# Quartered first loads and a swapped-operand gate product in a three-layer sequence-256 kernel

## The reference, cut to what matters

```python
proj = x @ w_in                      # x: 256 x 1024, w_in: 1024 x 8208
h_a, c_a, b_a, z_a, qkv, z_b, beta_raw, a_raw = jnp.split(proj, cuts, axis=-1)
qkv = jax.nn.silu(causal_depthwise_conv(qkv, conv_b_w))
beta = jax.nn.sigmoid(beta_raw)      # 8 columns, one for each head
g = -jnp.exp(a_log) * jax.nn.softplus(a_raw + dt_bias)   # 8 more columns
```

## Time and profile before

| what | value |
|---|---|
| runs | 1047.58, 1049.68, 1049.87 us (median 1049.68) |
| span of the profiled execution | 1048.4 us |
| what lies around the span | no separate time of the profiled execution is given; the median stands 1.28 us above its span |
| TensorE matmul / weight load busy | 97% / 86% of the span |
| VectorE / ScalarE busy | 72% / 51% |
| mean granted TensorE clock | 0.994 |

### The profile page before, as it was taken

The page is one execution under the profiler, slowest core; times in us unless marked ns, Lnnn a source line. Parts: engine busy times, 40 slices in busy tenths (PEclk is TensorE's granted clock), DMA queues, the critical chain, the costliest instruction groups (busy, mean ns, idle before and its releaser), DMA issues.

```text
span 1048.4 us, 21565 instructions
## 1 busy us (share of the span) xinstructions
PE 1019.6 (97%) x9120; PEld 897.6 (86%) x9120; DVE 752.1 (72%) x1049; ACT 530.2 (51%) x590; POOL 0.5 (0%) x7
## 2 busy tenths in 40 slices
PE   9999999999999999999999999989999999999998
PEld 7999999999866798989898787659986669999986
DVE  5999957678557668677787866867986775565553
ACT  5674544483353464435555433656687564335331
POOL 0000000000000000000000000000000000000000
PEclk8999999999999999999999999999999999999999
DMA  9454343244326664425343554876352446545441
GB/s 353 162 183 161 129 154 106 97 162 161 123 81 255 236 240 167 150 83 200 122 162 122 178 185 163 320 295 241 123 181 99 161 143 260 218 184 188 157 171 47
DMA packets 26302, 181.47 MB, mean 173 GB/s; under 512 B 3040, under 2 KB 3296, under 8 KB 4960
## 3 DMA queue, kind: packets, MB, share of 16 engines
q1 hardware_dynamic: 25056, 174.66, 45.2%
q10 hardware_dynamic: 1152, 5.45, 1.4%
HBM read 179.04 MB, written 1.05 MB: 172 GB/s over the span
## 4 chain that ended last, share of the span: by engine, by line
PE 87%; DVE 7%; ACT 3%; DMA 2%; issue 1%; SPq 0%; DVEq 0%; ACTq 0%
PE PS L916 84%; DVE WL L1799 2%; DMA RAW<-wst 1%; ACT WH L1386 1%; PE PS L1079 1%; DMA layer<-xt 1%; DVE X L1995 1%; DVE X L1996 1%; PE PS L1157 1%; PE PS L1307 0%; DVE STAT L1977 0%; DVE X L1976 0%; DVE layer_ln L2109 0%; DVE layer L2102 0%; ACT block L1690 0%
## 5 line engine op out<-in xcount | busy, mean ns | idle before, releaser
L916 PE MATMUL PS<-XTH,WH 128*128 128x256 f32 x1392 | 403.7, 290 | 6.2 <-issue 1.5
L916 PE MATMUL PS<-XTL,WH 128*128 128x256 f32 x1392 | 394.8, 284 | 0.0
L916 PE MATMUL PS<-XTH,WL 128*128 128x256 f32 x1392 | 394.7, 284 | 0.0
L1799 DVE TENSOR_TENSOR WL<-RAW,WH 128x2048 fp32r<-128x2048 f32 x138 | 314.2, 2277 | 99.8 <-ACT WH L1386 96.4
L1386 ACT ACTIVATE WH<-RAW 128x2048 fp32r<-128x2048 f32 x138 | 262.7, 1904 | 214.2 <-PE PS L916 208.7
L916 PEld LDWEIGHTS PS<-XTH,WH 128*128 128x128 f32 x1392 | 267.8, 192 | 12.6 <-issue 3.8
L916 PEld LDWEIGHTS PS<-XTL,WH 128*128 128x128 f32 x1392 | 268.0, 193 | 1.6 <-issue 1.4
L916 PEld LDWEIGHTS PS<-XTH,WL 128*128 128x128 f32 x1392 | 267.8, 192 | 0.0
L916 PE MATMUL PS<-WH,YH 128*128 128x512 f32 x224 | 89.6, 400 | 1.1 <-DVE YL L2274 1.1
L916 PE MATMUL PS<-WH,YL 128*128 128x512 f32 x224 | 87.4, 390 | 0.0
L916 PE MATMUL PS<-WL,YH 128*128 128x512 f32 x224 | 87.3, 390 | 0.0
(11 more groups left out here) (293 smaller groups left out, 1112.6 us busy)
## 6 DMA issues: line engine op xcount, KB each, us to landing
RAW<-wst SPq DMA_DIRECT2D x162, 1024.0 KB, 4.9
LNW<-lnrow ACTq DMA_DIRECT2D x3, 1024.0 KB, 6.7
RAW<-wst SPq DMA_DIRECT2D x4, 512.0 KB, 5.7
layer<-xt SPq DMA_DIRECT2D x2, 512.0 KB, 5.3
XR<-x ACTq DMA_DIRECT2D x1, 1024.0 KB, 4.7
out<-X SPq DMA_DIRECT2D x4, 256.0 KB, 3.3
CST<-cst ACTq DMA_DIRECT2D x1, 640.0 KB, 8.7
PT<-pt SPq DMA_DIRECT2D x1, 512.0 KB, 5.6
```

Of the source, the lines that this page charges most:

```text
L916: return pe.matmul(o, lhsT, rhs, start=start, stop=stop)
L1799: tt(WL[:, i % RAW_RING, 0:n], RAW[:, i % RAW_RING, 0:n], as_float(WH[:, k % SPLIT_RING, 0:n]), ALU.subtract).then_inc(vector_done, 1)
```

## The change

The diff changes the following things.

1. x and slab 0 are loaded in eight pieces of 256 KB (four each, in turn) in place of four of 512 KB. `xs` has four steps, and slab 0 is split by `top:0`, `top:1`, `top:2` and `split:0:0`. Unit k:0:0 waits for the pieces one by one.
2. The gate product is two steps. `baw` holds the gate weights still (two blocks side by side, 32 columns) in four column groups, with 512 columns of x moving: four float32 matmuls into PSUM bank 0, each output group a partial sum. ScalarE copies it to `BAW`. `ba` then adds up and transposes it by four float32 matmuls with `BAW` stationary and a 0/1 matrix `PICK` of 16 columns moving, into bank 1. `PICK` is made by VectorE in the new step `pick` by two `tensor_reduce` over parts of `ident`, behind a wait for `CST`.
3. `baw` is TensorE's first step, `ba` stands behind `k:0:0`. On VectorE the order is `xs:3 split:0:0 split:1:1 split:2:2 pick ba k:0:0 split:3:3 ba1`; before it was `xs:0 ba split:1:1 split:2:2 ba1 k:0:0 split:3:3`.
4. Four matmuls of ones in place of six.
5. `ORDER_T` is a new sequence all through the kernel. `ORDER_S` and `ORDER_V` are the same as before behind the front (VectorE's from `split:3:3` on but for `ba1`).

```diff
     step("setup", on="SGV")
-    for half in range(2):
-        step("xs", half, on="SV")
+    step("pick", on="V")
+    for q in range(4):
+        step("xs", q, on="SV")
...
-    step("ba", on="TV", banks=(0,))
+    step("baw", on="TS", banks=(0,))
+    step("ba", on="TV", banks=(1,))
...
 ORDER_T = """
-ba first:k:0:0 k:0:0 first:k:0:1 k:0:1 first:v:0:0 v:0:0 norm:k:0 first:v:0:1 first:q:0:0 v:0:1 gcc q:0:0 first:q:0:1
-q:0:1 first:zb:0:0 zb:0:0 gc:0 first:zb:0:1 zb:0:1 first:k:1:0 k:1:0 norm:q:0 vtr:0 first:k:1:1 k:1:1 first:v:1:1
...
-ab:0:1 gv:0:0 ah:1:0 gx:0:5:1 gs:0 first:ac:1:0 gu:0:6:1 gks:0 ac:1:0 gv:0:1 first:az:1:0 go:0 az:1:0 gr:0:0
-first:zb:1:0 first:ab:1:0 ab:1:0 zb:1:0 gc:1 first:ah:1:1 first:zb:1:1 zb:1:1 vtr:1 norm:q:1 first:ac:1:1 ah:1:1
...
-gu:1:3:0 gp:1:3:1 gx:1:2:1 gx:1:3:0 gp:1:4:0 gu:1:3:1 gu:1:4:0 gp:1:4:1 gx:1:3:1 gx:1:4:0 gp:1:5:0 gu:1:4:1 gu:1:5:0
...
-hm:0:6 first:q1:1:0 hc:0 q1:1:0 ho:0 first:q1:1:1 q1:1:1 hr:0:0 hd:1 first:i:1:0 first:f:2:0 i:1:0 first:i:1:1 hm:1:0
-first:f:2:1 hm:1:1 i:1:1 f:2:0 hm:1:2 f:2:1 hm:1:3 first:z1:1:0 z1:1:0 hm:1:4 first:z1:1:1 z1:1:1 first:q1:2:0 hm:1:5
...
-gate:1:0:1 first:gate:1:1:0 adat:6 first:gate:1:1:1 gate:1:1:0 gate:1:1:1 ada:7:0 ada:7:1 ada:9:0 ada:9:1 ada:4:0
-adat:7 xt:4:1 xt:4:0 xt:4:2 xt:4:3 adat:9 ada:4:1 first:feat:8 gates:0 feat:8 gates:1 first:feat:0 qn:1:2 gcol feat:0
...
+baw first:k:0:0 k:0:0 ba first:k:0:1 k:0:1 first:v:0:0 v:0:0 first:v:0:1 norm:k:0 v:0:1 first:q:0:0 gcc first:q:0:1
+gc:0 q:0:0 q:0:1 first:zb:0:0 zb:0:0 first:zb:0:1 zb:0:1 first:k:1:0 k:1:0 norm:q:0 vtr:0 first:k:1:1 k:1:1 first:v:1:0
...
+gp:0:6:1 ab:0:1 gv:0:0 ah:1:0 gs:0 gu:0:6:1 first:ac:1:0 gks:0 ac:1:0 gv:0:1 first:az:1:0 go:0 az:1:0 gc:1 gr:0:0
+first:ab:1:0 ab:1:0 first:zb:1:0 zb:1:0 first:zb:1:1 zb:1:1 first:ah:1:1 first:ac:1:1 vtr:1 norm:q:1 ah:1:1 ac:1:1
...
+gx:1:2:1 gp:1:3:1 gx:1:3:0 gp:1:4:0 gu:1:3:1 gu:1:4:0 gx:1:3:1 gp:1:4:1 gx:1:4:0 gp:1:5:0 gu:1:4:1 gu:1:5:0 gx:1:4:1
...
+hm:0:6 first:q1:1:0 hc:0 q1:1:0 ho:0 first:q1:1:1 q1:1:1 hr:0:0 hd:1 i:1:0 first:i:1:0 first:i:1:1 first:f:2:0 hm:1:0
+i:1:1 hm:1:1 first:f:2:1 f:2:0 hm:1:2 f:2:1 hm:1:3 first:z1:1:0 z1:1:0 hm:1:4 first:z1:1:1 z1:1:1 hm:1:5 first:q1:2:0
...
+gate:1:0:1 first:gate:1:1:0 adat:6 first:gate:1:1:1 gate:1:1:0 gate:1:1:1 ada:7:0 ada:9:0 ada:7:1 ada:9:1 adat:7
+ada:4:0 xt:4:1 xt:4:0 xt:4:3 xt:4:2 ada:4:1 adat:9 first:feat:8 gates:0 feat:8 gates:1 first:feat:0 qn:1:2 gcol feat:0
...
-            for half in range(2):
-                k, n = slice(4 * half, 4 * half + 4), slice(half * HALF // 2, (half + 1) * HALF // 2)
-                sp.dma_start(XT0[:, k, :], xt_in[:, k, :]).then_inc((x_loaded, rest_loaded)[half], 16)
-                sp.dma_start(RAW[:, 0, n], wst[0, :, n]).then_inc((top_loaded, slab_loaded[0])[half], 16)
+            for q in range(4):
+                k, n = slice(2 * q, 2 * q + 2), slice(q * SLAB, (q + 1) * SLAB)
+                sp.dma_start(XT0[:, k, :], xt_in[:, k, :]).then_inc(xt_loaded[q], 16)
+                sp.dma_start(RAW[:, 0, n], wst[0, :, n]).then_inc(top_loaded[q], 16)
...
+            def t_baw(step):
+                for q in range(4):
+                    pe.wait_ge(xt_loaded[q], 16)
+                pe.wait_ge(wba_loaded, 16)
+                for j in range(4):
+                    last = mm(PS[32 * j:32 * (j + 1), 0, :], flat(WBA[:, 2 * j:2 * j + 2, :]), tiles(XT0, 2 * j, 2))
+                last.then_inc(tensor_done, 1)
+
             def t_ba(step):
-                pe.wait_ge(x_loaded, 16)
-                pe.wait_ge(rest_loaded, 16)
-                pe.wait_ge(wba_loaded, 16)
+                pe.wait_ge(scalar_done, scalar_at("baw"))
+                pe.wait_ge(vector_done, vector_at("pick"))
                 for c in range(NT):
-                    for k in range(KC):
-                        last = mm(PS[:, 0, c * 16:(c + 1) * 16], XT0[:, k, c * P:(c + 1) * P], WBA[:, k, :],
-                                  start=k == 0, stop=k == KC - 1)
+                    for k in range(2):
+                        last = mm(PS[:, 1, c * 16:(c + 1) * 16], BAW[:, k * T + c * P:k * T + (c + 1) * P], PICK[:, k, :],
+                                  start=k == 0, stop=k == 1)
...
-            for _ in range(6):
+            for _ in range(4):
                 mm(PS[:, 7, :], ONES[:], ONES[:].unsqueeze(1).to_broadcast([P, 4, P]))
...
+            def s_baw():
+                act.wait_ge(tensor_done, tensor_at("baw"))
+                fn(BAW, PS[:, 0, :], ACT.Copy).then_inc(scalar_done, 1)
...
+            def v_pick():
+
+                dve.wait_ge(cst_loaded, 16)
+                every = ident.rearrange("p (j a i) -> p a i j", j=4, a=2)
+                for a in range(2):
+                    last = dve.tensor_reduce(PICK[:, a, :], every[:, a], AX.X, ALU.add)
+                last.then_inc(vector_done, 1)
```

More of the change, by code:

```diff
@@ L508 @@
[L508 to L512, removed]
@@ new lines @@
+gp:1:5:1 gx:1:5:0 gp:1:6:0 gu:1:5:1 gu:1:6:0 gp:1:6:1 gx:1:5:1 gv:1:0 out:0:1:1 gs:1 gu:1:6:1 gks:1 out:0:0:2 gv:1:1
+go:1 gr:1:0 gr:1:1 pl:0:0 out:0:1:2 first:out:0:0:3 first:out:0:1:3 out:0:0:3 out:0:1:3 xt:0:0:0 pl:0:1 ada:0:0
+xt:0:0:1 ada:0:1 xt:0:1:0 ada:1:0 adat:0 ada:1:1 xt:0:1:1 first:gate:0:0:0 first:gate:0:0:1 gate:0:0:0 gate:0:0:1
+first:gate:0:1:0 adat:1 ada:2:0 xt:1:0 xt:1:1 first:gate:0:1:1 gate:0:1:0 gate:0:1:1 ada:2:1 first:f:0:0 xt:1:2 xt:1:3
+adat:2 first:f:0:1 f:0:0 f:0:1 first:q1:0:0 q1:0:0 first:q1:0:1 q1:0:1 first:i:0:0 hd:0 i:0:0 first:f:1:0 hm:0:0
@@ L516 @@
+down:1:4 first:down:1:5 down:1:5
 """
 ORDER_S = """
[L518 to L526, removed]
@@ L527 @@
-split:41:46 ada:1:1 split:42:47 xt:0:1:1 first:gate:0:0:1 split:43:48 gate:0:0:1 first:gate:0:1:1 split:44:51 xt:1:0
-xt:1:1 gate:0:1:1 split:45:52 ada:2:1 split:46:53 xt:1:3 xt:1:2 f:0:0 split:47:54 f:0:1 split:48:55 split:49:56 q1:0:0
-q1:0:1 split:50:57 split:51:58 split:53:60 f:1:0 split:52:59 i:0:1 split:54:61 split:55:62 f:1:1 split:56:63 hc:0
-z1:0:0 z1:0:1 split:57:64 q1:1:0 hq:0:0 q1:1:1 split:58:65 hr:0:0 split:59:66 split:60:67 f:2:0 split:61:68 i:1:1
+setup xs:0 top:0 xs:1 top:1 xs:2 top:2 xs:3 split:0:0 split:1:1 baw split:2:2 split:3:3 ba1 k:0:0 split:4:4 k:0:1
@@ new lines @@
+first:out:0:0:3 c1 first:out:0:1:3 lna:0:0 lnb:0:0:0 out:0:0:3 out:0:1:3 xt:0:0:0 lna:0:1 lnb:0:0:1 lnb:0:1:0
+split:40:45 lnb:0:1:1 xt:0:0:1 split:41:46 adat:0 xt:0:1:1 xt:0:1:0 split:42:47 first:gate:0:0:1 split:43:48 gate:0:0:1
+adat:1 first:gate:0:1:1 split:44:51 xtl:1:0 xtl:1:1 gate:0:1:1 split:45:52 lb2 adat:2 xtl:1:3 xtl:1:2 split:46:53 f:0:0
+split:47:54 f:0:1 split:48:55 split:49:56 split:50:57 hy:0:0 hd:0 hy:0:1 hp:0:0 split:51:58 hy:0:2 hp:0:1 split:53:60
+hy:0:3 split:52:59 f:1:0 hy:0:4 hp:0:3 hp:0:2 hy:0:5 hp:0:4 hy:0:6 split:54:61 hy:0:7 hp:0:6 hp:0:5 split:56:63
@@ L591 @@
+split:126:152 split:125:151 ff:18 split:127:153 ff:19 split:128:154 split:129:155 split:130:156 split:131:157 ff:20
+split:132:158 ff:21 split:133:159 first:down:0:5 split:134:160 down:0:5 split:135:161 split:136:162 split:137:163
+split:138:164 first:down:1:5 down:1:5
 """
@@ L949, in features @@
             def features(step, ready):
-                if step.slabs[0] == 0 and step.half == 0:
-                    pe.wait_ge(vector_done, vector_at("split_top"))
-                else:
+                if step.slabs[0]:
                     split_ready(step.slabs[0])
```

197 lines of the change are left out of this document (105 added, 92 removed).

## The result

The changed kernel takes 1054.86 us (median of 4 runs, 1053.78 to 1055.45) against 1048.71 for the kernel before (4 runs, the three shown and 1047.74): ratio 1.0052, 95% interval 1.0037 to 1.0067. 1051.5 was forecast, and 1054.86 lies 0.7 us above the upper edge of the stated range (1054.2). Its profiled execution has a span of 1053.6 us and took 1055.45. In every run with both numbers the whole time is 1.74 to 1.88 us above the span, so the profiled execution of before took 1050.2, some 1.5 above the median; the 1.28 that I put between span and median was too small. I compare spans: 1050.2 forecast, 1053.6 measured, 5.2 above before.

A forecast was written before the change was run, and what follows sets the result against it. TensorE, busy for 1019.6 of 1048.4 us, was taken as the bound. Front +2.2, kinds of array +3.1 and waits -3.5 made +1.8: span 1050.2, plus 1.28 to the median, 1051.5 us; range 1047.0 to 1054.2.

The forecast's parts named there:

- no change: Whole kernel: 1051.5 us forecast, a difference that can't be told; own range 1050.2 to 1053.0, chance 0.42.
- front: Up to k:0:1: early k:0:0 given back waiting for pick, +0.2; ba at half clock +0.5; clock fall +1.5; sum +2.2 us.
- kinds of array: Delta rule, both groups: ten more pairs of changes between small-array and full-array steps at 0.31 us each, +3.1 us.
- 213 us: Wait of 0.78 us at 213.37: zb:1:1 now stands in front of ah:1:1, -0.8 us.
- 463 us: Wait of 1.25 us at 463.57: i:1:1 goes in front of f:2:1, but hm:1:1 waits for VectorE, -0.8 us.
- 698 us: Wait of 3.04 us at 697.96, ended by the slab's landing: adat:7 goes into it, -1.0 us.
- 747 us: Wait of 1.22 us at 747.12: feat:4 goes before feat:6, but the wait comes back some steps later, 0.
- attention (804 us): Wait of 1.03 us at 803.83: ada:5:0, 0.9 us long, goes into it, -0.9 us.
- VectorE's lag: Rival, up to 120 us: VectorE falls over 1.5 us behind TensorE, waits cost +2.7, 1054.2 us; chance 0.18.
- The clock holds: Rival, front: k:0:0 at half clock fills the time to 20.6, front only +0.2, 1049.5 us; chance 0.18.
- Faster: Rival: clock holds and most changes of kind fall into short waits, +0.5 for 3.1, 1046.9 us; chance 0.22.
- It doesn't do what it says: Rival, front: no earlier start of k:0:0, pieces slower by 1 us, pick moves to 21.6; 1052.5 us, inside the forecast's range.

The follow-up runs named there:

- half_loads: Changed kernel with x and slab 0 loaded in four pieces of 512 KB as before; 1.0042 of the kernel before, span 1053.5.
- old_levels: Changed kernel with the two stretches of the delta rule's levels in the old order; 1.0020 of the kernel before, span 1049.2.
- pairs_back: Changed kernel with the attention stretch (first:val:0:0 to score:15) in the old order, except ada:5:0 before turn:7; 1.0044 of the kernel before, span 1051.3.
- sequence_alone: Kernel before with TensorE's new sequence from v:0:0 on behind its old front; 1.0004 of the kernel before, span 1047.2.
- front_alone: Changed kernel with TensorE's old sequence behind the new front; 1.0062 of the kernel before, span 1051.9.
- front_again: The same kernel as front_alone, run once more for a second trace; 1.0045 of the kernel before, span 1049.9.
- ba_late: Changed kernel with ba behind k:0:1 on TensorE and behind split:3:3 on VectorE; 1.0022 of the kernel before, span 1050.7.
- the two padded ones: best and the changed kernel, each with ten more matmuls of ones of 16 columns; 0.9950 and 1.0062 of the kernel before.
- best: Changed kernel with pick before split:2:2, and the old order in the levels, at ho:2 and for score and pv pairs; 0.9972 of the kernel before.
- best_padded: best with ten more matmuls of ones of 16 columns behind the four of 512; 0.9950 of the kernel before, median 1044.52 us.
- pick_early: Changed kernel with pick in front of split:2:2 on VectorE, nothing else; 1.0018 of the kernel before, span 1050.2.
- old_with_pick: best without the five eased waits, so TensorE's old order from gc:0 to the end; 1.0002 of the kernel before.

## Why the prediction was right or wrong

The likeliest case was "no change"; it is slower, 3.4 us above the forecast by spans. Term by term, by the table:

| term | forecast | measured | where |
|---|---|---|---|
| front | +2.2 | +2.76 | v:0:0 |
| kinds of array | +3.1 | +2.87 | groups 0 and 1 |
| 213 us | -0.8 | -0.95 | gs:0 to gk:1 |
| 463 us | -0.8 | -0.69 | hm:1:0 to hm:2:0 |
| 698 us | -1.0 | -0.64 | ada:4:0 to first:feat:8 |
| 747 us | 0 | -0.94 | first:feat:8 to qn:1:0 |
| attention (804 us) | -0.9 | +2.01 | qn:1:0 to first:out2:0:1 |
| not foreseen | | +0.84 | the rest |

*Front.* The mechanism was the one forecast: the early start of k:0:0 is given back whole in the wait of `ba` for `pick`. Four sizes were off. "I take 0 for slabs 1 and 2" was wrong: slab 2 is taken up at 16.73 in place of 15.80 (+0.9), and half_loads shows that the pieces do it. In 14 us from the start the changed kernel has moved 4.38 MB, the one before 4.68 and half_loads 4.63. The bound of +1.0 held for slab 2 and not for slab 1 (13.05 in place of 11.73), on which nothing hung. `ba` did not run at the half clock (-0.5). The lone fall of the clock cost 1.47 of 1.5. The last quarter of x landed at 10.1 and not at 8.5, and `baw` took 1.9 at the half clock, so that the start at 9.5 became 11.96; it cost nothing, covered by the wait. (With its own terms, the lower bound of the front is -0.2 and not -0.4.)
The Trainium skill (DMA: Bandwidth & Descriptors, Bandwidth) spoke against the quarters; I set its rule aside for the row of 430 GB/s, and the runs bear out its direction, though not its size.

*Kinds of array.* Right in cause and near in size; old_levels shows it, 0.14 us a change. The count of 104 and 124 holds for the small steps of the two layers alone: over all of TensorE's steps the changes of array form are 157 and 192. Of the 15 more that were left out, 8 are at `ada` steps and 6 at `pv`.

*Waits.* Three right within 0.4 us. At 747 us "it comes back some steps later" was wrong: 0.9 stayed. The wait at 804 us, put at -0.9, gave some 0.1 and stands in the sum for attention.

*Attention* is the step that failed by the traces, with 2.9 of the 3.4 us: -0.9 was forecast, +2.01 measured. The prediction put only ada:5:0 into the wait at 803.83. It counted changes of kind in the delta rule and did not ask in the new order which steps had lost a neighbour. Three pairs of `pv` are taken apart (3 x (1.60 - 1.07) = 1.6), so is the pair score:15, score:14 (0.84), and the pairs score:5, score:6 and score:7, score:8 take 0.27 and 0.25 longer (0.5): 2.9. The wait of 1.0 is gone, but the two ada:5 steps apart and adat:5 cost 0.25 more each, and small shifts give 0.4 back: +2.0. pairs_back and the other traces show it.

*Not foreseen:* the step out:1:0:0 takes 0.79 longer, 0.46 of it a stop. There is also a new wait of 0.95 at ho:2, because first:q1:3:1 no longer stands between hc:2 and ho:2, so ScalarE's copy of hc:2 is uncovered; other steps there gain, and of it 0.24 is left at i:3:0. The rest are shifts of a few tenths.

*By the times of the runs* the miss lies elsewhere, and the table alone would hide it. The new sequence by itself can't be told from the old one (sequence_alone 1.0004, +0.4 us), near its forecast of -0.4. The front alone costs 4.7 to 6.5 us (1.0045 and 1.0062), where +2.2 was forecast. Beside the 2.6 of its trace, the stop (1.1) and the larger share of half clock (1.2) are in no term of the prediction. For the sequence, the dearer pairs are set off by a smaller share of half clock (1.6), also in no term. That the sequence came out as forecast is luck. These intervals are some 1 to 1.6 us wide to each side, and which share of the clock belongs to which cause is not shown.

*The rivals.* VectorE's lag did not decide at +2.76: front_alone and front_again have no wait for it behind `ba`. ba_late shows that it is real, but only when TensorE is over 1.5 us ahead of the kernel before, and not late. "The clock holds" was wrong. (The row given for it, 8.44 to 11.86, shows the full clock in the gate product and not in the ones.) "Faster" asked for a clock that holds and changes of kind that cost 0.5; they cost 2.87. "It doesn't do what it says" was half true: k:0:0 gained 1.1 us and not 3.5.

What stays open: in which stretches the slowest runs of the kernels with the new front lose their 2 us more, and how much of the sequence's clock gain is more than chance.

## What to carry to other kernels

Work brought forward in a strict list is worth only what the next blocking operand allows: find out when that comes (here 21.5 us), move that first (one place in VectorE's list gave 3.4 us), and expect a long wait to be paid twice, once as the wait and once at the half clock behind it. When a sequence is rearranged, compare which small-array steps still stand next to their partner, not only how often the kind of array changes. A difference of 0.2% can hang on where the clock falls and on where in the program a step lies. So compare several traces before it is given a cause, and hold the sum of one trace against the times of all runs.

## What was not expected of the hardware

*The stop without a wait.* All ten traces with the new front and no padding stop for 0.46 to 1.33 us inside out:1:0:0; neither kernel with the old front does, nor the two padded ones. One packet of an instruction queue (16 KB) moves shortly before, here in 606.9 to 607.2 us of the changed kernel and in 602.4 to 602.6 of best (queue, packets, MB, share):

```profile
q8 instruction: 1, 0.02, 20.3%
```

```profile
q8 instruction: 1, 0.02, 29.3%
```

The stop ends 2.2 to 2.4 us behind that packet in all ten traces (607.0 and 609.25, 602.5 and 604.75, 605.5 and 607.83, 603.7 and 606.09 in four of them). But a packet alone is not enough: the kernel before has one at 605.1, also beside slab loads, and best_padded one at 601.3, and no stop follows. What sets the ten apart is the next packet of that queue. It comes 4.0 to 4.8 us behind the first in the ten, and 14.3 to 14.6 us behind it in the four without a stop. (Such a close pair stands elsewhere too, in the kernel before at 590.7 and 595.5, without a stop.) So it looks like a fetch of code that arrives late; that ten matmuls more remove the stop is shown, that it is the fetch is inferred.
The Trainium skill (Runtime: NRT & Kernel Launch, Instruction fetch mechanics) says that code streams in by blocks and that crossing a block's end is mostly hidden. If the stop is such a crossing, then it is not hidden here, for up to 1.33 us (front_alone).

*The clock behind a wait.* In eight traces `ba` waits for 1.86 to 4.41 us, and in all eight the clock was then half: for 3.41 us behind waits of 1.86, 2.99, 3.00 and 3.08, for 6.83 us behind 1.88, 2.73, 4.23 and 4.41. The length of the wait does not say which. Behind 0.41 us or none (pick_early, ba_late, best_padded, old_with_pick) it stayed full. A single stretch over full-array products cost 1.5, a double one 2.9 to 3.0 with `ba`'s own share (from `ba` to v:0:0 it takes 9.69 us in half_loads and 6.65 in pick_early). Where a double one begins in the wait itself it costs less: in front_alone it ran from 18.84 to 25.66, and the front was +2.64.
